# Opening stage of a two-block transformer step: sixteen modulation slabs with places of their own, multiplied to columns on TensorE

## The reference, cut to what matters

```python
c_act = jax.nn.silu(c)
mod = jnp.einsum('bd,de->be', c_act, w_ada[l]) + b_ada[l]
sh1, sc1, g1, sh2, sc2, g2 = jnp.split(mod[:, None, :], 6, axis=-1)
h = rms_norm(x, g_pre_mix[l]) * (1.0 + sc1) + sh1
proj = jnp.einsum('bsd,de->bse', h, w_in[l])
```

## Time and profile before

| | us |
|---|---|
| median of 3 runs | 2835.41 |
| lowest, highest | 2828.34, 2836.82 |
| the profiled execution | 2827.46 |
| its span | 2825.7 |
| TensorE busy in it | 2715.6 |
| VectorE, ScalarE, GpSimd busy | 1873.3, 1329.0, 271.7 |
| mean granted TensorE clock | 0.988 |

### The profile page before, as it was taken

One profiled execution on the slowest core, in us unless ns is written; L12 is line 12 of the kernel. 1 busy time (PEld: TensorE's weight loads), 2 busy tenths in 40 slices (PEclk: granted clock), 3 DMA queues, 4 the chain that ended last, 5 costly groups with the idle time before them and its releaser, 6 DMA issues. The chain is left out here.

```text
span 2825.7 us, 41859 instructions
## 1 busy us (share of the span) xinstructions
PE 2715.6 (96%) x16730; PEld 2135.1 (76%) x16730; DVE 1873.3 (66%) x2844; ACT 1329.0 (47%) x1939; POOL 271.7 (10%) x429
## 2 busy tenths in 40 slices
PE   7999989999999999999999999889899999999998
PEld 4757644777888888867778887767778878888886
DVE  7678987568666466684777616755756576656676
ACT  4246765468555434463441114452324565543344
POOL 0115640001000000000000001110000110000000
PEclk9999999999999999999999999999999999999999
DMA  7721100346566888732463341206233656677884
GB/s 269 227 69 38 49 1 1 135 148 229 208 234 224 298 280 293 256 114 73 125 153 124 129 143 55 82 29 229 88 121 128 215 209 223 224 296 258 292 285 156
DMA packets 205906, 474.01 MB, mean 168 GB/s; under 512 B 49040, under 2 KB 69648, under 8 KB 199376
## 3 DMA queue, kind: packets, MB, share of 16 engines
q1 hardware_dynamic: 187792, 393.73, 42.1%
q0 software_dynamic: 17920, 77.61, 7.0%
HBM read 344.09 MB, written 124.29 MB: 166 GB/s over the span
## 5 line engine op out<-in xcount | busy, mean ns | idle before, releaser
L2151 PE MATMUL psum<-merged_operand 128*128 128x512 f32 x1536 | 360.7, 390 | 0.0
L2151 PEld LDWEIGHTS psum<-merged_operand 128*128 128x128 f32 x1536 | 288.3, 188 | 60.7
L2151 PE MATMUL psum<-h_half_operand 128*128 128x512 f32 x1344 | 316.8, 391 | 0.0
L2151 PEld LDWEIGHTS psum<-h_half_operand 128*128 128x128 f32 x1344 | 252.3, 188 | 55.5 <-issue 1.0
L2151 PE MATMUL psum<-h_half_operand,weight_parts_operand 128*128 128x512 f32 x768 | 177.5, 392 | 0.8 <-DVE weight_parts_operand L2657 0.6
L2151 PEld LDWEIGHTS psum<-h_half_operand,weight_parts_operand 128*128 128x128 f32 x768 | 143.5, 188 | 34.1 <-DVE weight_parts_operand L2657 2.7
L3626 PE MATMUL psum<-x_operand,weight_high 128*128 128x512 f32 x448 | 141.9, 398 | 2.1 <-DVE z_mixed L3254 2.1
L3626 PE MATMUL psum<-o_operand,weight_high 128*128 128x512 f32 x448 | 138.3, 390 | 0.0
L3626 PE MATMUL psum<-x_operand,weight_low 128*128 128x512 f32 x448 | 138.0, 389 | 0.0
L2657 DVE TENSOR_TENSOR weight_parts_operand<-weight_ring,weight_parts_operand 128x1024 fp32r<-128x1024 f32 x66 | 80.7, 1223 | 85.0 <-ACT weight_parts_operand L2307 84.8
L215 DVE CAST weight_high<-weight_ring 128x1024 fp32r<-128x1024 f32 (+1 forms) x52 | 30.3, 583 | 157.0 <-PE psum L3626 96.3
(11 more groups left out here) (651 smaller groups left out, 5972.2 us busy)
## 6 DMA issues: line engine op xcount, KB each, us to landing
o<-in_w_ff SPq DMA_DIRECT2D x80, 512.0 KB, 4.5
merged<-hidden_terms SPq DMA_DIRECT2D x56, 512.0 KB, 5.8
hidden_upper<-in_w_ff_down SPq DMA_DIRECT2D x48, 512.0 KB, 4.9
weight_ring<-in_w_out SPq DMA_DIRECT2D x32, 512.0 KB, 3.5
hidden_terms<-weight_parts POOLq DMA_DIRECT2D x16, 1024.0 KB
hidden_terms<-weight_ring POOLq DMA_DIRECT2D x16, 1024.0 KB, 8.0
hidden_upper<-in_w_ff_up SPq DMA_DIRECT2D x32, 512.0 KB, 4.5
o<-hidden_terms SPq DMA_DIRECT2D x28, 512.0 KB, 5.6
```

The source lines that it names most:

```text
L2151: mm = pe.matmul(bank, w[:, at:at + P], tiles(r, i), start=opens and m == 0, stop=closes and m == 2, skip_group_check=resumed)
```

## The change

- Slabs 0 to 15 get a place each in `mod_slabs`, a buffer of 16 x 1024 numbers per partition, which lies where `h_high` and `h_low` of the next stage will be. Their loads, and those of the next stage's first four weight slabs into the ring, wait for nothing any more.
- `x` is loaded in four quarters of two tiles each, with a signal each.
- `sq` has five places instead of two.
- TensorE takes slabs 5, 7, 9, 11, 13 and 14 and multiplies them with the slab as stationary operand and one column of `silu(c)` moving (`add_columns`), eight matmuls for a slab, straight to columns in PSUM banks 2 and 3. VectorE takes the other ten: 0 to 4, 6, 8, 10, 12 and 15. `part` is added behind slab 9, `second` at the end, both in the same form. The row, its copies and its turning are gone.
- VectorE scales tiles 0 and 1 behind slab 6, 2 and 3 behind slab 8, 4 behind 10, 5 behind 12, 6 behind 15, and 7 among the last steps. Of those it now applies four (0, 2, 4, 7), ScalarE four (1, 3, 5, 6).
- `stay_busy` issues 12 matmuls instead of 14.
- Sixteen semaphores are added, one for each slab.

```diff
+    SCALED_BEHIND = {6: (0, 1), 8: (2, 3), 10: (4,), 12: (5,), 15: (6,)}
+    by_pe, FIRST_ENDED_BEHIND = (5, 7, 9, 11, 13, 14), 9
+    by_dve = [s for s in range(LATER) if s not in by_pe]
...
-        part, row, sq = room[:, 0, :], room[0:1, 1, :], room[:, 2:4, :]
+        part, sq = room[:, 0, :], [room[:, n, :] for n in (1, 2, 3, 8, 9)]
...
-                for half in range(2):
-                    tiles = slice(4 * half, 4 * half + 4)
-                    sp.dma_start(x[:, tiles, :], of[:, tiles, :]).then_inc(landed[half].sem, 16)
+                for q in range(4):
+                    tiles = slice(2 * q, 2 * q + 2)
+                    sp.dma_start(x[:, tiles, :], of[:, tiles, :]).then_inc(landed[q].sem, 16)
                 for s in range(LATER):
-                    if s >= RING:
-                        wait_emptied(sp, s - RING)
-                    sp.dma_start(K.ring[:, s % RING, :], K.dram["w_ada"][s]).then_inc(K.slab_loaded[s % RING].sem, 16)
+                    sp.dma_start(slab(s), K.dram["w_ada"][s]).then_inc(slab_landed[s], 16)
...
-                def add_to_row(standing, moving, first, last):
-                    for h in range(2):
-                        mm = pe.matmul(psum[0:1, 2 + h, :], standing, moving[:, h * HALF:(h + 1) * HALF], start=first,
-                                       stop=last)
+                def add_columns(bank, of, by, first, last):
+                    for t in range(KT):
+                        mm = pe.matmul(psum[:, bank, t:t + 1], of[:, t * P:(t + 1) * P], by, start=first and t == 0, stop=last,
+                                       skip_group_check=True)
...
-                add_slab(by_pe[0])
-                pe.wait_ge(slab_added.sem, KT)
-                for t in range(KT):
-                    mm = pe.matmul(psum[:, 6, t:t + 1], part[:, t * P:(t + 1) * P], K.const("ones")[:, 0:1],
-                                   start=True, stop=True)
-                mm.then_inc(K.pe_done.sem, 1)
-                for s in by_pe[1:]:
+                for s in by_pe:
                     add_slab(s)
+                    if s == FIRST_ENDED_BEHIND:
+                        pe.wait_ge(slab_added.sem, len([n for n in by_dve if n < KT]))
+                        add_columns(2, part, K.const("ones")[:, 0:1], False, True).then_inc(K.pe_done.sem, 1)
                 pe.wait_ge(slab_added.sem, len(by_dve))
-                add_to_row(K.const("ones")[:, 0:1], second, False, True)
-                for t in range(KT):
-                    if t % 4 == 0:
-                        pe.wait_ge(row_kept.sem, row_kept.n + t // 4 + 1)
-                    mm = pe.matmul(psum[:, 7, t:t + 1], row[:, t * P:(t + 1) * P], K.const("ones")[0:1, 0:1],
-                                   start=True, stop=True)
-                mm.then_inc(K.pe_done.sem, 1)
-                K.stay_busy(pe, 0, 14)
+                add_columns(3, second, K.const("ones")[:, 0:1], False, True).then_inc(K.pe_done.sem, 1)
+                K.stay_busy(pe, 0, 12)
...
-                for i in range(KT + 2):
+                for i, s in enumerate(by_dve):
                     add_slab(i)
-                scale(0)
-                for i in range(KT + 2, len(by_dve)):
-                    add_slab(i)
-                for t in range(1, KT):
-                    scale(t)
+                    for t in SCALED_BEHIND.get(s, ()):
+                        scale(t)
...
-                for t in (0, 2, 4, 6, 7):
+                for t in (0, 2, 4, 7):
+                    if t == 7:
+                        scale(t)
+                        c.wait()
...
-                for h in range(2):
-                    act.wait_ge(K.pe_done.sem, pe0 + 2 + h)
-                    act.activation(row[:, h * HALF:(h + 1) * HALF], psum[0:1, 2 + h, :], ACT.Copy).then_inc(row_kept.sem, 1)
-                for t in (1, 3, 5):
+                for t in (1, 3, 5, 6):
                     shifted(t)
```

More of the change, by code:

```diff
@@ L370, in reduce_angle, with opening @@
     c(dve.tensor_scalar(out, out, PI_IN, -PI_IN, op0=ALU.min, op1=ALU.max))
-def opening(nc, K, x, of, cos, sin, room, w_val):
+def opening(nc, K, x, of, cos, sin, room, slab_room, w_val):
     LATER = 2 * KT
-    FIRST_BY_PE, ALTERNATE = KT + 1, 3
+    SCALED_BEHIND = {6: (0, 1), 8: (2, 3), 10: (4,), 12: (5,), 15: (6,)}
+    by_pe, FIRST_ENDED_BEHIND = (5, 7, 9, 11, 13, 14), 9
+    by_dve = [s for s in range(LATER) if s not in by_pe]
     psum = K.psum
@@ L398, in opening, with slab @@
         _, after = K.turn_of_ring()
-        by_pe = [s for s in range(FIRST_BY_PE, LATER) if (s - FIRST_BY_PE) % 2 == 0 or s > FIRST_BY_PE + 2 * (ALTERNATE - 1)]
-        by_dve = [s for s in range(LATER) if s not in by_pe]
         at = {}
[L403 to L410, removed]
+        def slab(s):
+            return slab_room[:, s, :]
         with nc.Block(no_gpsimd_drain=True) as block:
@@ L432, in _ @@
             def _(pe):
[L433 to L438 removed]
+                def add_columns(bank, of, by, first, last):
+                    for t in range(KT):
+                        mm = pe.matmul(psum[:, bank, t:t + 1], of[:, t * P:(t + 1) * P], by, start=first and t == 0, stop=last,
+                                       skip_group_check=True)
                     return mm
                 def add_slab(s):
[L442 to L444 removed]
+                    pe.wait_ge(slab_landed[s], 16)
+                    add_columns(2 + s // KT, slab(s), silu_c[:, s % KT:s % KT + 1], s in (by_pe[0], first_later), False)
+                first_later = [s for s in by_pe if s >= KT][0]
                 pe.sem_inc(K.slab_used.sem, RING)
@@ L452, in _ @@
                     for h in range(2):
[L453 removed]
+                        mm = pe.matmul(psum[:, 4 + h, :], K.const("ones"), sq[t % len(sq)][:, h * HALF:(h + 1) * HALF],
                                        start=(t == 0), stop=(t == KT - 1))
@@ L481, in add_slab @@
                     k, to = s % KT, part if s < KT else second
-                    wait_slab(dve, s)
-                    w = K.ring[:, s % RING, :]
-                    if i in (0, KT):
+                    dve.wait_ge(slab_landed[s], 16)
+                    w = slab(s)
+                    if s in (0, KT):
                         ins = dve.tensor_scalar(to, w, silu_c[:, k:k + 1], None, op0=ALU.mult)
@@ L539, in _ @@
                 act.activation(silu_c[:], K.col("c", 0, KT), ACT.Silu).then_inc(K.act_done.sem, 1)
-                act.activation(row[:, 0:1], K.col("eps")[0:1], ACT.Ln)
+                act.activation(cos[0:1, 0:1], K.col("eps")[0:1], ACT.Ln)
                 for t in range(KT):
[L542 to L545, removed]
+                    act.wait_ge(landed[t // 2].sem, landed0[t // 2] + 16)
+                    if t >= len(sq):
+                        act.wait_ge(K.sq_used.sem, sq_used0 + t - len(sq) + 1)
+                    act.activation(sq[t % len(sq)], x[:, t, :], ACT.Square).then_inc(K.sq_ready.sem, 1)
                 act.wait_ge(K.sq_used.sem, sq_used0 + KT)
@@ L5145, in build @@
                 cos, sin, packed = (K.sbuf(angles, name, [P, S]) for name in ("cos", "sin", "rot_rows"))
+                w_val = score[:, 0:KT * 136].rearrange("p (k f) -> p k f", k=KT)
+                with ExitStack() as inner:
+                    opening(nc, K, merged, x_t, cos, sin, rot, K.sbuf(inner, "mod_slabs", [P, 2 * KT, S]), w_val)
                 with ExitStack() as inner:
                     parts = K.pair(inner, "h", [P, KT, S])
-                    w_val = score[:, 0:KT * 136].rearrange("p (k f) -> p k f", k=KT)
-                    opening(nc, K, merged, x_t, cos, sin, rot, w_val)
                     rotate_and_score(nc, K, merged, parts, rot, cos, sin, packed, score[:, 0:S], score, val, w_idx, w_val, bits)
```

20 lines of the change are left out of this document (8 added, 12 removed).

## The result

| | before | after |
|---|---|---|
| median of 16 runs each, us | 2833.24 | 2838.07 |
| lowest, highest | 2828.34, 2837.0 | 2831.6, 2844.35 |
| ratio after / before, 95% interval | | 1.0018 [1.0010, 1.0025] |
| profiled execution and its span | 2827.46, 2825.7 | 2844.35, 2842.6 |
| mean granted TensorE clock | 0.988 | 0.98 |

The change makes the kernel 0.18% slower, about 5 us (2.8 to 7.1). That is less than the 0.3% that I had allowed for as no change, but the interval of this measurement is tighter and leaves 1.0 out. The profiled execution of after is the slowest of its 16, and that of before was faster than all 16 of its own, so the 16.9 us between the two are not what the change does.

The account below looks back on a forecast made before the run. TensorE was taken as the bound, its one-column groups slowed by a fallen clock; value matmuls start at 55.4 instead of 52.45, 3.0 us later, and 2831.9 plus 3.0 gives 2834.9, put as 2835; range 2827 to 2844.

Parts of the forecast that it names:

- The base: Whole kernel: the middle of four executions shown, 2831.9 us, to which 3.0 us of slowing was added.
- a group of columns at the lower clock: Opening, TensorE: 16 one-column records at 1.2 GHz take 3.1 us, or 3.4 at 0.213 a record.
- Granted clock 0.50 from about 30 to beyond 49: Opening: sign that TensorE's clock falls during the one-column groups and stays low past 49 us.
- VectorE idle for 3 us: Opening: sign that VectorE waits 3 us for the root before scaling tile 0.
- slab 15 would have had 4.7 us to spare: End of the opening: TensorE is the bound, so slab 15 could come 4.7 us later at no cost.
- The step from line 1004 to the opening: Opening: one-column groups lower the clock as at line 1004, where it fell 3.6 us after wide matmuls.
- the first rival: Opening: the clock holds, VectorE is the bound, value matmuls start at 49.0, 3.4 us earlier; 2828.5 us, chance 0.18.
- The second rival: Border to the value matmuls: the low clock goes on into them, 6.7 us late in all; 2838.6 us, chance 0.20.
- The sum: Whole kernel: value matmuls start 3.0 us later, at 55.4, giving 2834.9, put as 2835 us.
- there is slack in the loads: Opening before the change: slab 15 was there by about 42.2, while turning the row started only at 45.98.
- The quarters: Opening: the first quarter of x arrives 2.5 us earlier, squares end at 26.8 instead of 29.4, root at about 30.4.
- The third rival: Opening: SyncE's queue holds loads back, slab 15 comes at 42.2, time as forecast; its chance is within the forecast's 0.62.

Follow-up runs that it names:

- e0: The changed kernel, unaltered, run once more: value matmuls start at 57.86, 2836.32 us.
- e1: The changed kernel with 128 columns moving instead of one in the column matmuls: start 49.94, ratio to the kernel before 0.9993.
- e7: e6 with one column moving again in the column matmuls instead of 128: start 55.53, ratio to the kernel before 1.0014.
- e6: e1 with slabs, sums, scalings and applied tiles shared anew between TensorE, VectorE and ScalarE: ratio to the kernel before 0.9978.
- e3: The kernel before with only a place for each of the 16 slabs and all loads issued at once: start 48.62, ratio 0.9989.
- e4: The kernel before with only x in four quarters and four places for squares: start 57.16, ratio 1.0009.
- e2: The changed kernel with slabs 5 and 7 given to VectorE, so six one-column groups on TensorE: start 55.53, ratio to the kernel before 1.0020.

## Why the prediction was right and where it was wrong

It was right in the mechanism and wrong in the side: 2835.0 stood 0.4 us under the median before, 2835.41, the kernel became slower, and 2838.07 is 3 us above the forecast. The steps that failed are two terms of the sum. The base, 2831.9, was the middle of four executions and not the median with which the result was compared, and this turned 3.0 us of slowing into none. And a group of columns at the lower clock was put at 3.1 us where it takes 3.41: over five groups that is 1.6 us, the largest part of what separates the 3.0 us of slowing from the 5.4 of e0.

**The clock.** "Granted clock 0.50 from about 30 to beyond 49", "VectorE idle for 3 us", "the last columns starting straight behind slab 14's", "slab 15 would have had 4.7 us to spare": all are in the rows of after (31.5 to 58.8; 3.81 us; 49.59 right behind slab 14; slab 15 added at 43.4, 6.2 us before its group starts at 49.59). The step from line 1004 to the opening carried. e1 and e7 show that the width of the moving operand is the cause, which was only argued before: the first rival, clock holds, came about for such groups only where 128 columns moved. The rule of the Trainium skill, "TensorE: Matmul & The Clock Gate", section "Why this matters for your kernels", that a TensorE kept busy goes to the full clock and holds it, agrees with e1 and e6 (1.00 from 36 to 40) and not with after and e7 (0.50 in the same windows, busy without a gap).

**The size of a group at the lower clock.** This is the term that was mis-sized. I took 0.193 us a record, from 30 records of line 1004 ahead of the clock's fall and 34 behind it, and named 0.213, its last rows, as the other end. The 30 are what 0.12 us a record gives for the time up to 253.4; they are not a count. The two windows of line 1004 in the kernel before say otherwise (window, us, busy and count of PE and PEld, granted clock, DMA share, GB/s; a record that crosses an edge is counted in both):

```profile
249.75:253.40 3.65, 3.65 (x34) 3.65 (x33) 0.99 0.00 0
253.40:259.97 6.57, 6.57 (x32) 6.57 (x32) 0.50 0.00 0
```

Some 33 records came ahead and 31 behind, and 6.57 / 31 is 0.212. After shows 10.24 us for 48 records (39.35 to 49.59), 0.213 each, 3.41 a group. Five groups at +0.31 are 1.6 us. Against e0, to keep after's late `x` out:

| step | predicted | e0 | difference |
|---|---|---|---|
| squares end | 26.8 | 27.4 | +0.6 |
| slabs 5, 7, 9 | 7.0 | 7.5 | +0.5 |
| the five other groups | 15.5 | 17.1 | +1.6 |
| from there to the value matmuls | 6.1 | 5.9 | -0.2 |
| value matmuls start | 55.4 | 57.9 | +2.5 |

The last rows of line 1004, which lie at one clock, were the better source. The squares were late by the slow start told below. The clock fell when expected: 30.7 forecast, 30.3 in e0, 31.5 in after with its late `x`.

**The second rival** was right in half: the columns took 0.213, and `stay_busy` 5.47 us, the late end of 2.9 to 5.8. Its other half did not come about, and only just: the clock came back at 58.8 in after, 0.1 us ahead of the value matmuls (0.59 in the last window shown above), at 57.6 in e0, 0.3 us ahead, and in e7 0.2 us behind. The 128 value matmuls of after took 15.06 us as they do in e6 at full clock. So it is luck that this rival's centre, 2838.6, lies so near the 2838.07 measured.

**The sum.** e0's start is 5.4 us late and after's 6.4, where 3.0 were forecast. The ratio gives 5.1 (0.0018 x 2833.24), with 2.8 to 7.1: it agrees with the start. By this measure the forecast of 3.0 us was on the right side and too small.

**The base.** That 3.0 us of slowing came out as "2835, about the median before" is the second fault. I put the sum on the middle of the four executions, 2831.9, to undo a lucky profile, but the number against which it is read is the median shown, 2835.41, of three. 16 runs gave 2833.24; my middle was 1.3 below it. A difference should have been put on the median it is compared with: 2838.4. That this is so near the 2838.07 measured is chance, since the median of three was itself 2.2 high; with 5.4 in place of 3.0 it would have been 2840.8. The range, 2827 to 2844, held the result.

**What I costed at nothing.** "Before, slab 15 is used by TensorE ... so there is slack in the loads" was right for the end of the queue and missed its middle: the wait for slab 9 stopped TensorE and took the clock with it, and doing away with it is worth 3.8 us (e3). The quarters, for which I booked 2.5 us of earlier root, widen that same pause and cost 4.7 us alone (e4), some of it a later slab 9. In the whole change the first of these is drowned: by e1, loads, quarters and sharing with wide sums come to 2.5 us less than before; the single column takes back 7.9.

**The third rival**, loads held back, didn't happen. The issue of the 16 slabs took SyncE 18.9 us, but they moved at 408 to 414 GB/s. Slab 15 landed at about 38.6 (issued at 23.0, 15.6 us to landing) where 37.3 was forecast, and VectorE took it at 42.13.

**Left open.** Later stages shift between executions by several us either way: at 1700 to 1710 before ran at a clock of 0.80, e0 at 0.66 and after at 0.53. The windows, with the same columns as above.

Before:

```profile
1700.00:1710.00 10.00, 10.00 (x204) 9.05 (x202) 6.87 (x12) 2.13 (x4) 1.77 (x1) 0.80 0.01 3
```

After:

```profile
1700.00:1710.00 10.00, 6.37 (x136) 5.02 (x136) 3.02 (x7) 1.20 (x2) 0.00 (x0) 0.53 0.01 2
```

The same work stands a few us apart in them, so they do not compare the same instructions. e3's equal starts with totals 11.7 us apart say that most of it is scatter. From the start of the value matmuls to the end of the span the fourteen profiled executions took 2773 to 2786 us. The five that started latest (55.5 to 58.9) lie in the middle of that, at 2775 to 2784, so no sign is seen that a late start costs more than itself; so few executions cannot exclude it.

## What to carry to other kernels

A matmul that feeds one column through a full 128 x 128 load is as cheap as 128 columns while the clock is up, and in the long stretches here in which nothing else ran (after, e7, line 1004) it let the clock fall; broadcast the moving operand to the full width, which cost room in PSUM and no time here (0.12 us a record either way). Before moving work earlier on TensorE, ask what stands between it and the next piece: an earlier end with the same next arrival is a longer pause, and the clock that falls in it is paid by everything behind. And put a forecast difference on the median with which it will be compared, not on a middle of one's own.

## What the runs showed of the hardware that I had not expected

- TensorE busy 1.00 in every window is no sign that the clock holds: after, 27 us at 0.50 without a gap. The page's busy time goes up and hides it; the count of records a window shows it, 11 against 5 or 6.
- Wide moving operands did not always bring the clock back. In e4 it stayed at 0.50 for 12 us of work, of which 3.5 us at first and 5.3 at the end were rows with 512 columns moving over a one-column stationary operand; in the kernel before it was back at 34.9, 3.5 us into the same rows. And `stay_busy`, 128 columns moving as in e1, stood at 0.50 from its start at 53.00 to its end in after. The width that held the clock in e1 did not bring it back there.
- The first squares run at half pace at a granted clock of 1.00: 3 records in 2 us and later 6, that is a record each 0.85 us and then each 0.43. These are the paces of 512-column records at 0.50 (0.89 in e4) and at 1.00 (0.44 in e3), so the clock may have been low there without the profile's column showing it; no run here tells. The slow part ends between 14 (e2) and 18 (after, before), whether the squares begin at 10.6 or at 13.1, so the same 32 records take 15.5 to 17.1 us. Windows of after, TensorE alone (window, us, busy and count, granted clock, DMA share, GB/s):

```profile
12.00:14.00 2.00, 2.00 (x3) 1.00 1.03 412
...
18.00:20.00 2.00, 2.00 (x6) 1.00 1.02 408
```

- SyncE issues loads that wait for nothing at the pace of the transfers. Its row in the timeline of after:

```profile
5.19 18.87 SPq L417 DMA_DIRECT2D mod_slabs<-in_w_ada  x16
```

16 issues in 18.87 us are 1.2 us each, where 512 KB at 410 GB/s take 1.28. Each landed 14.3 to 16.8 us after its issue. What stood behind them in that queue had to wait too, with no wait written.
